# Seven half-size products in place of eight for x, B and C of a state-space layer

## The reference

```python
def mamba2_mixer(x, w_in, conv_w, conv_b, dt_bias, a_log, d_skip, norm_w, w_out):
    zxbcdt = x @ w_in
    z = zxbcdt[..., :SSM_D_INNER]
    xbc = zxbcdt[..., SSM_D_INNER:SSM_D_INNER + SSM_CONV_DIM]
    ...
    xbc = jax.nn.silu(causal_depthwise_conv(xbc, conv_w, conv_b))
    ...
    y = ssd_chunked(xh, dt, a, bm, cm) + ...
    ...
    return yg.astype(x.dtype) @ w_out
```

## Time and profile before

| | |
|---|---|
| Time, median of 3 runs | 1807.79 us (1807.18 to 1809.17) |
| Span of the profiled execution | 1806.1 us |
| TensorE busy with matmuls | 1786.0 us, 99% |
| VectorE, ScalarE, GpSimd busy | 721.9, 448.2 and 70.9 us |
| Loads | 527.41 MB, 292 GB/s on average |
| State-space stage with its output projection | about 0 to 261 us |
| First expert stage | about 271 to 703 us |

### The profile page before, as it was taken

The page is one execution under the profiler, slowest core; times in us unless marked ns, Lnnn a source line. Parts: engine busy times, 40 slices in busy tenths (PEclk is TensorE's granted clock), DMA queues, the critical chain, the costliest instruction groups (busy, mean ns, idle before and its releaser), DMA issues.

```text
span 1806.1 us, 21261 instructions
## 1 busy us (share of the span) xinstructions
PE 1786.0 (99%) x8612; PEld 984.0 (54%) x8647; DVE 721.9 (40%) x1667; ACT 448.2 (25%) x958; POOL 70.9 (4%) x66
## 2 busy tenths in 40 slices
PE   9999999999999999999999999999999999999999
PEld 8888754443443333455444344343366767568874
DVE  3566754212221213035421221221345566234675
ACT  2332312111111100133210111110134534217780
POOL 0000000000000000000000000000011110001110
PEclk9999999999999999999999999999999999999999
DMA  9723569999999999708899999999942332041520
GB/s 389 305 83 139 193 254 410 420 427 428 426 428 429 427 427 425 309 1 349 357 425 428 428 427 427 428 427 427 425 162 94 140 123 110 7 181 47 236 91 23
DMA packets 41828, 527.41 MB, mean 292 GB/s; under 512 B 4800, under 2 KB 5472, under 8 KB 8576
## 3 DMA queue, kind: packets, MB, share of 16 engines
q1 hardware_dynamic: 39200, 516.70, 68.7%
q10 hardware_dynamic: 2528, 9.31, 1.3%
HBM read 524.91 MB, written 1.08 MB: 291 GB/s over the span
## 4 chain that ended last, share of the span: by engine, by line
PE 88%; DMA 9%; DVE 2%; SPq 1%; ACT 0%; issue 0%; POOL 0%; DVEq 0%; ACTq 0%
PE ps L212 32%; PE ps L876 20%; PE ps L911 10%; DMA ring<-in_wu 6%; PE ps L810 4%; PE ps L928 3%; PE ps L715 2%; DMA ring<-in_w_lat 2%; PE ps L1702 2%; PE ps L1670 2%; PE ps L1234 1%; PE ps L679 1%; PE ps L1717 1%; PE ps L883 1%; PE ps L1446 1%; PE ps L1459 1%
## 5 line engine op out<-in xcount | busy, mean ns | idle before, releaser
L876 PE MATMUL ps<-ring,work 128*64 128x512 f32 x1856 | 409.1, 593 | 6.0 <-DMA ring<-in_wu 5.7
L212 PE MATMUL ps<-xl,ring 128*128 128x256 f32 (+3 forms) x1344 | 291.5, 375 | 0.4 <-DMA ring<-in_w_x 0.4
L876 PEld LDWEIGHTS ps<-ring,work 128*64 128x64 f32 x1856 | 131.6, 137 | 270.7 <-issue 251.2
L212 PEld LDWEIGHTS ps<-xl,ring 128*128 128x128 f32 x1344 | 243.7, 190 | 39.5 <-issue 2.5
L911 PE MATMUL ps<-ring,work 128*64 128x512 f32 x816 | 181.5, 594 | 0.1
L212 PE MATMUL ps<-ring,xl 128*128 128x256 f32 (+1 forms) x576 | 176.0, 463 | 0.2 <-ACT xl L1787 0.2
L2647 DVE TENSOR_TENSOR work<-work,ps 128x512 f32<-128x512 f32 x32 | 22.0, 688 | 361.4 <-PE ps L876 341.7
L212 PEld LDWEIGHTS ps<-ring,xl 128*128 128x128 f32 x576 | 108.3, 190 | 59.3 <-issue 49.9
L911 PEld LDWEIGHTS ps<-ring,work 128*64 128x64 f32 x816 | 56.2, 137 | 100.3 <-issue 98.7
L3178 POOL TENSOR_TENSOR small<-small,halves 128x1 f32<-128x1 f32 (+4 forms) x42 | 45.7, 1087 | 1545.7 <-DVE small L2449 936.6
L2608 DVE SCALAR_TENSOR_TENSOR work<-ps,small,big 128x512 f32<-128x512 f32 x60 | 45.0, 750 | 135.8 <-ACT big L1918 135.8
(11 more groups left out here) (476 smaller groups left out, 1958.9 us busy)
## 6 DMA issues: line engine op xcount, KB each, us to landing
ring<-in_wg SPq DMA_DIRECT2D x62, 2048.0 KB, 20.6
ring<-in_wu SPq DMA_DIRECT2D x52, 2048.0 KB, 21.7
ring<-in_wd SPq DMA_DIRECT2D x48, 2048.0 KB, 22.0
xl<-in_wd SPq DMA_DIRECT2D x10, 2048.0 KB, 23.5
xl<-in_wu SPq DMA_DIRECT2D x9, 2048.0 KB, 19.1
ring<-in_w_odd SPq DMA_DIRECT2D x8, 2048.0 KB, 7.4
ring<-in_w_xz SPq DMA_DIRECT2D x7, 2048.0 KB, 22.9
ring<-in_w_qkv SPq DMA_DIRECT2D x6, 2048.0 KB, 34.3
```

Source lines behind the costliest of these rows:

```text
L212: i = e.matmul(bout, lhs(k), rhs(k), start=start and k == ks[0], stop=stop and k == ks[-1])
L876: last = e.matmul(b[64 * j:64 * j + 64, :], x[:, 4 * a + k, 64 * j:64 * j + 64], w[k // 2][:, 2 * (k % 2) + j, :], start=a + k == 0, stop= ...
```

## The change

For groups 2 to 7 each half is computed in seven products in place of eight. A half is split in two along the features of the result, in two along the tokens and in two along the 1024 inputs, so it is a product of 2x2 blocks. Seven products of blocks, each of 4 matmuls with 128 columns, replace the 16 matmuls with 256 columns (`tensor_seven`). They need sums and differences of weight blocks: four operations of GpSimd for each half (`pool_sums`, 128 partitions by 512 numbers each, one of them in place in the ring), issued two groups ahead and, from group 3 on, behind `mm_conv` of the group before, whose products read the same areas. Four sums of x blocks are formed once (`pool_x_sums`). In GpSimd's order the sums of group g+2 stand ahead of the root of group g.

The seven results lie in two banks, ps[5] and the half's own. VectorE copies one and adds the others up (5 more operations for a half) into an area `raw` of SBUF, and the convolution reads from there. Its second block for half 1 is moved behind the product that raises `gated`.

The weight sums need a buffer of the ring ("half", held until `mm_conv(7, 1)`), so that 7 are left for the loads; "sum" is given its buffer later, and two of the output weights change places.

```diff
--- before.py
+++ after.py
@@ -16,6 +16,7 @@
 U16 = mybir.dt.uint16

 NSLOT = 8
+FAST = 2
 BESIDE, TAIL = (8, 0), (15, 1)
 PARTED, EARLY = ("mu", 2, 1), ("mu", 0, 1, 0)
 ASIDE = [("mg", 0, 1), ("md", 0, 1)]
...
@@ -374,10 +379,15 @@
             ring.add(("w", g), 1, mm_z(g))
             if g % 2 == 0:
                 ring.add(("BC", g // 2), 1, mm_conv(g + 1, 1))
-        ring.add(("sum",), 0, out_mm("p5"))
-        WO = [(0, 0, "c21"), (1, 1, "p3"), (0, 1, "p7"), (1, 0, "p4")]
+            if g == 1:
+                ring.add(("half",), 0, mm_conv(7, 1))
+                ring.order.remove(ring.chunks["half",][0])
+        WO = [(0, 0, "c21"), (0, 1, "p7"), (1, 1, "p3"), (1, 0, "p4")]
         for hf, n, last in WO:
+            if (hf, n) == (1, 0):
+                ring.add(("sum",), 0, out_mm("p5"))
             ring.add(("wo", hf, n), 1, out_mm(last))
+        ring.order.insert(1, ring.chunks["half",][0])

         def ring_moe(l):
             ring.last(NSLOT)
@@ -446,6 +456,19 @@
+        halfv = ring.view("half")
+        wsums = [area(halfv, 1536 * i, (3, 4, 128)) for i in range(2)]
+        xsums = [area(xl, 2048, (4, 128)), area(xl, 2560, (4, 128)), area(halfv, 3072, (4, 128)), area(halfv, 3584, (4, 128))]
+        raw = area(big, 3584, (4, 128))
+
+        def wq(g, half, j, h_):
+            v = kview(8, 512)(ring.view("BC", g // 2) if half else ring.view("w", g))
+            c = 256 * j + 128 * (g % 2) if half else 256 + 128 * j
+            return v[:, 4 * h_:4 * h_ + 4, c:c + 128]
+
+        def xq(h_, c):
+            return xS[:, 4 * h_:4 * h_ + 4, 128 * c:128 * c + 128]
+
         def ya(t, hf):
             return ygT[:, hf:14:2, t * 128:(t + 1) * 128]

@@ -589,7 +612,9 @@
             wv = kview(8, 512)(ring.view("w", g))
             wb = kview(8, 512)(ring.view("BC", g // 2))
             half, j = part // 2, part % 2
-            if half < 2:
+            if half < 2 and g >= FAST:
+                tensor_seven(e, g, half, j)
+            elif half < 2:
                 w0 = kview(8, 128)(ring.view("w", 0)[:, 1024 * j:1024 * j + 1024])
                 lw = (wv[:, :, 256 + 128 * j:384 + 128 * j] if g else w0) if half == 0 else \
                     wb[:, :, 256 * j + 128 * i:256 * j + 128 * i + 128]
@@ -617,6 +642,34 @@
                                lambda k: wv[:, k, 0:256], range(8))
                 if j == 1:
                     last.then_inc(*mm_z.up(g))
+
+        def tensor_seven(e, g, half, j):
+
+            x, y = ps[5], ps[2 + half]
+            s1, s2, s4 = (wsums[half][:, i] for i in range(3))
+            t1, t2, t3, t4 = xsums
+
+            def product(b, at, w, x_):
+                for k in range(4):
+                    last = e.matmul(b[:, 128 * at:128 * at + 128], w[:, k, :], x_[:, k, :], start=k == 0, stop=k == 3)
+                return last
+
+            if j == 0:
+                e.wait_ge(*(ring("BC", g // 2) if half else ring("w", g)))
+                if half:
+                    e.wait_ge(*first_sums(g, 0))
+                else:
+                    e.wait_ge(*(first_sums(g - 1, 1) if g > FAST else dec_d(0, 1)))
+                product(x, 0, wq(g, half, 0, 0), xq(0, 0))
+                product(x, 1, wq(g, half, 0, 1), xq(1, 0))
+                e.wait_ge(*sums_in(g, half))
+                product(x, 2, s2, t2).then_inc(*part_mm.up(g, half))
+            else:
+                e.wait_ge(*conv(g - 1, half))
+                product(y, 1, s1, t1)
+                product(y, 2, wq(g, half, 1, 0), t3)
+                product(y, 0, wq(g, half, 1, 1), t4)
+                product(y, 3, s4, xq(1, 1)).then_inc(*mm_conv.up(g, half))

         def tensor_first_gate(e):

@@ -2241,14 +2294,30 @@
             scalar_odd(e)


-        def vector_conv(e, g, half):
-
+        def vector_conv(e, g, half, blocks=(0, 1)):
+
+            if g >= FAST and 0 in blocks:
+                x = ps[5][:, :].rearrange("p (a n) -> p a n", a=4)
+                y = ps[2 + half][:, :].rearrange("p (a n) -> p a n", a=4)
+                e.wait_ge(*part_mm(g, half))
+                e.tensor_copy(raw[:, 1], x[:, 0]).then_inc(*vs.up())
+                e.wait_ge(*vs())
+                e.tensor_tensor(raw[:, 0:4:2], bc(raw[:, 1], 1, 2), x[:, 1:3], ALU.add).then_inc(*first_sums.up(g, half))
+                e.wait_ge(*first_sums(g, half))
+                e.wait_ge(*mm_conv(g, half))
+                e.tensor_tensor(raw[:, 1:4:2], bc(raw[:, 2], 1, 2), y[:, 1:3], ALU.add).then_inc(*vs.up())
+                e.wait_ge(*vs())
+                e.tensor_tensor(raw[:, 1], raw[:, 1], y[:, 3], ALU.add).then_inc(*vs.up())
+                e.tensor_tensor(raw[:, 2:4], bc(raw[:, 3], 1, 2), y[:, 0:2], ALU.add).then_inc(*vs.up())
+                e.wait_ge(*vs())
             e.wait_ge(*mm_conv(g, half))
             if g:
                 e.wait_ge(*cs_in(g - 1))
-            for j in range(2):
+            for j in blocks:
                 blk = 2 * g + j if half == 0 else 16 + 8 * j + g
                 b = ps[2 + half][:, j * 256:(j + 1) * 256]
+                if g >= FAST:
+                    b = raw[:, 2 * j:2 * j + 2].rearrange("p a n -> p (a n)")
                 o = cv[:, 2 * half + j, :]
                 e.tensor_scalar(o, b, C("conv_w", 4 * blk + 3), C("conv_b", blk), ALU.mult, ALU.add).then_inc(*vs.up())
                 for s in range(1, 4):
@@ -2388,7 +2457,7 @@
                     e.tensor_tensor(dec[:, t], dec[:, t], bc(ps[1][:, 128 + 128 * t:256 + 128 * t], 1, 4),
                                     ALU.mult).then_inc(*(vs.up() if t == 0 else dec_in.up(g)))
                 if g < 7:
-                    vector_conv(e, g + 1, 1)
+                    vector_conv(e, g + 1, 1, (0,))
                 else:
                     vector_mix(e)
                 e.wait_ge(*mm_y(g))
@@ -2406,6 +2475,8 @@
                 e.wait_ge(*vs())
                 e.wait_ge(*zs_in(g))
                 e.tensor_tensor(yv, yv, zs[:, i], ALU.mult).then_inc(*gated.up(g))
+                if g < 7:
+                    vector_conv(e, g + 1, 1, (1,))
                 e.wait_ge(*y_sq(g))
                 e.tensor_scalar(rsg[:, 0:2], ssq[:, 0:2], 1.0 / 256, EPS1, ALU.mult, ALU.add).then_inc(*y_var.up(g))
                 e.wait_ge(*gated(g))
@@ -3177,8 +3248,37 @@
             e.wait_ge(*before)
             e.tensor_tensor(x, x, n[0:x.shape[0]], ALU.pow).then_inc(*done)

+        def pool_x_sums(e):
+
+            t1, t2, t3, t4 = xsums
+            e.wait_ge(x_in[0], 16)
+            e.wait_ge(x_in[1], 16)
+            e.tensor_tensor(t1, xq(0, 1), xq(0, 0), ALU.subtract).then_inc(*gs.up())
+            e.wait_ge(*gs())
+            e.tensor_tensor(t2, xq(1, 1), t1, ALU.subtract).then_inc(*gs.up())
+            e.tensor_tensor(t3, xq(1, 1), xq(0, 1), ALU.subtract).then_inc(*gs.up())
+            e.wait_ge(*gs())
+            e.tensor_tensor(t4, xq(1, 0), t2, ALU.subtract).then_inc(*sums_in.up("x"))
+
+        def pool_sums(e, g, half):
+
+            s1, s2, s4 = (wsums[half][:, i] for i in range(3))
+            e.wait_ge(*(ring("BC", g // 2) if half else ring("w", g)))
+            if g > FAST:
+                e.wait_ge(*mm_conv(g - 1, half))
+            e.tensor_tensor(s1, wq(g, half, 1, 0), wq(g, half, 1, 1), ALU.add).then_inc(*gs.up())
+            e.wait_ge(*gs())
+            e.tensor_tensor(s2, s1, wq(g, half, 0, 0), ALU.subtract).then_inc(*gs.up())
+            e.tensor_tensor(wq(g, half, 1, 0), wq(g, half, 0, 0), wq(g, half, 1, 0), ALU.subtract).then_inc(*gs.up())
+            e.wait_ge(*gs())
+            e.tensor_tensor(s4, wq(g, half, 0, 1), s2, ALU.subtract).then_inc(*sums_in.up(g, half))
+
         def gpsimd(e):
+            pool_x_sums(e)
             for g in range(8):
+                if g + 2 < 8:
+                    for half in range(2):
+                        pool_sums(e, g + 2, half)
                 pool_rsqrt(e, rsg[:, 0:2], y_var(g), y_rs.up(g))
             pool_rsqrt(e, mst[0:16, 0:1], z_var(0, 2), z_rs.up(0, 2))
             for t in range(2):
```

More of the change, by code:

```diff
@@ L279, in build @@
         qkT_in = Sig(sem("qkT_in"), qkT_mm.keys)
-        sc_mm, sc_max, sc_exp = sig("sc_mm", H8, range(2)), sig("sc_max", H8), sig("sc_exp", H8, range(2))
+        part_mm = sig("part_mm", range(FAST, 8), range(2))
+        first_sums = sig("first_sums", range(FAST, 8), range(2))
+        sc_mm, sc_max, sc_exp = then(part_mm, H8, range(2)), then(first_sums, H8), sig("sc_exp", H8, range(2))
         p_in, pT_mm, pT_in, av_mm, av_in = (sig(n, H8) for n in ("p_in", "pT_mm", "pT_in", "av_mm", "av_in"))
-        sl_var, sl_rs, sl_in = (sig(n, range(2), range(2)) for n in ("sl_var", "sl_rs", "sl_in"))
+        sums_in = Sig(sem("sums_in"), [("x",)] + each(range(FAST, 8), range(2)))
+        sl_rs = then(sums_in, range(2), range(2))
+        sl_var, sl_in = (sig(n, range(2), range(2)) for n in ("sl_var", "sl_in"))
         oT_mm, oT_in = sig("oT_mm", range(2), range(2)), sig("oT_in", range(2), range(2))
```

## The result

The changed kernel takes 1844.05 us (median of 4 runs, 1842.89 to 1845.85) against 1807.61 us before: ratio 1.0202, 95% interval 1.0190 to 1.0215. It is slower by 36.4 us, where 4.2 were forecast, and far outside the range of 1803 to 1818. The profiled execution has a span of 1842.3 us (1806.1 before).

The account below looks back on a forecast made before the run. It took TensorE as only just the bound in the state-space groups and loads as the bound in the first expert stage. 1806.1 - 7.7 (products) + 11.9 (loads) = 1810.3 us, plus 1.7 around it: 1812.0 us, range 1803 to 1818.

Parts of the forecast that it names:

- term 1: State-space halves on TensorE: 28 matmuls of 128 columns at 0.224 us take 6.27 us, saving 7.7 us over 12 halves.
- term 2: VectorE's five added operations a half: 0.4 us left before TensorE wants the product of the decays, cost 0.
- term 3: GpSimd's eight sums a group: 13.7 us with 3.3 of contention fit into 14.2 us, cost 0.
- (b): GpSimd's sums end late, 2 us in five groups, some 6 in all: 1818 us, chance 0.16.
- The clock behind a stop: At pair 0 TensorE may fall to 1.2 GHz after its new wait, costing 2.5 us (0 to 3.4).
- term 4: First expert stage's loads: a new wait of 11.4 us at pair 0, and the stage ends 11.9 us late.
- (c): The loads' lag is not paid and the state-space saving stands alone: 1800.1 us, chance 0.13.
- (d): State-space products of 128 columns cost 0.249 us each, so nothing is saved: 1819 us, chance 0.05.
- the stop at `big`: Sign: TensorE idle for some 11 us at the expert products' first use of `big`, ended by a DMA.
- the half rate behind it: Sign: matmuls at half rate behind the stop at `big`, or a granted clock under 1.00.
- the shift of all that follows: Sign: first expert stage ends some 4 us later, and all later stages are shifted by the same.
- the period of 23.8 us: Sign: state-space groups 1 to 6 have a period of 23.8 us in place of 25.1.

Follow-up runs that it names:

- J: Changed kernel without GpSimd's per-group sums (unsummed weights in their place) and with the ring's buffers in order of release: 1798.75 us, ratio 0.9952.
- A: Changed kernel with GpSimd's per-group sums left out, the products reading unsummed weights: 1811.78 us, ratio 1.0024.
- I: H with GpSimd's four sums of half 1 moved, two behind `gated` and two behind `y_norm`, the root between: 1807.86 us, ratio 1.0004.
- B: Changed kernel with VectorE writing the sums of the products to a PSUM bank, from which the convolution reads its first operand: 1817.16 us, ratio 1.0057.
- F: Changed kernel with 15 needless matmuls ahead of TensorE's wait for the product of the decays in groups 1 to 5: 1834.01 us, ratio 1.0146.
- C: Changed kernel with the ring's buffers given to the expert stage's loads in order of release, as before: 1831.26 us, ratio 1.0134.
- D: Changed kernel with both the convolution from PSUM (B) and the buffers in order of release (C): 1804.14 us, ratio 0.9982.
- H: D with VectorE's product of the decays put early, as in G: 1804.48 us, ratio 0.9983.
- E: Changed kernel with each of GpSimd's sums split into two operations of 256 columns: 1836.30 us, ratio 1.0159.
- G: Changed kernel with VectorE's product of the decays ahead of its wait for the second half of the products of x: 1835.06 us, ratio 1.0154.

## Why the prediction was wrong

**Products (term 1): right.** A half takes 6.25 us (6.27 forecast), 7.9 us for twelve. 0.2 us a group comes on top, the small waits at a group's end, for 9.1 in all (J: 9.1 under the 1807.9 of its chip).

**VectorE (term 2): hardly any spare time was right, the cost of 0 was not.** 0.4 us were forecast to be spare for the product of the decays. In A the product ends 0.26 to 0.29 us before TensorE goes on (0.06 in one group), and TensorE goes on 0.06 after it where it waits, so 0.2 are spare at most. Part of the miss is the tensor_scalar: from SBUF it takes 0.41 us where 0.35 was taken over from another operation, so it gives back 0.13 and not 0.19. "Each microsecond late is paid five or six times" was right: it was paid five times.

**GpSimd (term 3): the step that failed.** The prediction took the contention of the earlier trace rows as something that slows only GpSimd, and entered 3.3 us a group there, where it fitted. The runs show that VectorE pays, 3.56 us ahead of the product of the decays and 4.0 in the whole group, and VectorE had 0.2 to spare. That 3.3 and 3.56 lie close is chance: the forecast stretched GpSimd's sums over fourteen operations in proportion to elements, and the measured loss is five waits for a running sum. In the earlier trace rows the VectorE operation starts at 1719.63 and GpSimd's at 1720.14: GpSimd came second, so its row is the long one, as in I (2.56 us for a sum of 1.27). The rows show who waited when VectorE was first, and say nothing of the other order. In the changed kernel a sum is under way when the convolution begins, and VectorE comes second. By the Trainium skill (SBUF — State Buffer, Who interferes with whom) an operation of VectorE with two SBUF inputs and a GpSimd operation that reads SBUF exclude each other, and the order of issue decides which of them blocks until the other ends; the timelines of A, B and the changed kernel agree, with 0.48, 0.48 and 1.38 us a step. The prediction used the page on GpSimd alone. The remaining parts of the step held: a sum takes 1.27 us (1.25 forecast), and the root is not late (rival (b) falls: in the changed kernel VectorE's request ends at 112.66 us, and the root runs from 112.74 to 113.44).

**The clock behind a stop** was priced once, for pair 0, since no stop was foreseen in the groups. There it cost some 15 us (F, which fills the stops, is 10 us faster). At pair 0 2.60 us were measured and 2.5 forecast, a choice inside 0 to 3.4 that came out close.

**Loads (term 4): right, 1 us small at the end.** The stop is 10.24 us (11.4 forecast; the prediction's own terms, 289.2 - 277.87, give 11.3) and TensorE 13.0 behind (13.9). The last step, that the stream of loads had 2 us to spare and ends 11.9 late, failed: C, and the pairs B and D, A and J, show 12.8 to 13.0, so nearly all that is lost at pair 0 is lost in the end.

In the prediction's own terms the sum is then -9.1 + 17.2 + 15.2 + 12.8 = 36.1 us, where -7.7 + 11.9 stood and 36.4 were measured. The two terms in the middle are those of the failed step. Without them the forecast would have met its number: A, which leaves out only the sums, takes 1811.78 us where 1812.0 were forecast, though by two errors that largely cancel (1.4 us too little gained by the products, 0.9 too little lost by the loads). That the kernel is slower at all was forecast for the loads alone, and most of the loss has the other cause. None of the rivals held it. (c), that the lag is not paid, fell; (d) fell with the halves of 6.25 (by its own terms it is 1819.7, not 1819). Of the signs listed, the stop at `big`, the half rate behind it and the shift of all that follows came, though the expert stage ends 36.4 us later and not 4; the period of 23.8 us did not (26.7 to 31.5), and appears, at 23.56, only once the sums are out.

## What to carry to other kernels

When GpSimd gets work to do beside VectorE, list VectorE's operations in that stretch with all their tensors in SBUF, and charge each with the rest of a GpSimd operation, on VectorE's own path; reading one tensor from a PSUM bank took the charge away here, for 0.13 us an operation. A row that shows one of two engines stretched shows which came second, not which always pays. Time gained ahead of an operation that waits for a running sum is lost in that wait (H). Where an engine has only 0.2 us to spare, a stop can return in every turn of the loop, and on TensorE it can bring a fall of the clock with it.

## What the hardware did that was not expected

- The hold did not depend on the size of what was held: an operation on 128x2 took 0.81 us in place of 0.16 (I), one of 128x256 with a single tensor input 0.86 in place of 0.41 (changed kernel, L2322). When both queues were full they took turns: one VectorE step, one sum, 1.4 us a turn, and the sum was 0.2 us longer (1.45 for 1.27).
- Stops of 0.7 us (B, D) left the granted clock at 1.00; 2.4 us (E) and 3.2 us (changed kernel) brought 1.2 GHz behind them; 3.5 us in another place of the group (G) did not, in the profiled execution. Nor is the length alone what counts at the short end: 1.15 us (F) brought it, 1.33 us in the kernel before did not the earlier trace rows. What tells these apart was not tried and is open.
